# A hybrid decoder layer on one core: dt by column groups, and the samples' new states from stacked fp32r halves

## What is computed

```
u    = RMSNorm(x)
proj = u @ W_in                      # 2048 x 9248: z | xBC | dt (32 columns) | glu
dt   = softplus(dt_raw + dt_bias)    # one value per token and head, 32 heads
xBC  = SiLU(conv4(xBC)) -> x (32 heads of 64), B and C (4 groups of 128 states)
SSD scan, by heads:
  y = C h (decayed) + ((C B^T) * decay * dt) x
  new state of each sample and head: decay * h0 + sum_j B_j (decay_to_end * dt)_j x_j^T
  g = (y + D x) * SiLU(z), and group RMSNorm of g
conformer: GLU -> conv31 -> LayerNorm -> swish
x = x + RMSNorm(concat(ssd, conformer) @ W_out);  x = x + RMSNorm(W_down relu(W_up RMSNorm(x))^2)
```

## Time and profile before

| | |
|---|---|
| median of 3 runs | 1800.94 us |
| profiled execution, its own time | 1800.39 us |
| its span | 1798.8 us |
| PE (TensorE) busy | 1779.2 us, 99% |
| DVE (VectorE) busy | 1088.6 us, 61% |
| ACT (ScalarE) busy | 770.2 us, 43% |
| POOL (GpSimd) busy | 453.2 us, 25% |
| granted TensorE clock | 1.00 of full |
| DMA | 278.42 MB, 155 GB/s |

### The profile page before, as it was taken

The page is one execution under the profiler, slowest core; times in us unless marked ns, Lnnn a source line. Parts: engine busy times, 40 slices in busy tenths (PEclk is TensorE's granted clock), DMA queues, the critical chain, the costliest instruction groups (busy, mean ns, idle before and its releaser), DMA issues.

```text
span 1798.8 us, 34945 instructions
## 1 busy us (share of the span) xinstructions
PE 1779.2 (99%) x13213; PEld 1746.5 (97%) x13213; DVE 1088.6 (61%) x2004; ACT 770.2 (43%) x1139; POOL 453.2 (25%) x352
## 2 busy tenths in 40 slices
PE   8999999999999999999999999999999999999998
PEld 7999999999998898899899999999999999999998
DVE  5577887999788787865875333443434434344444
ACT  6443435555356565633443333333333333333442
POOL 1577776777651122222100000000000000000132
PEclk9999999999999999999999999999999999999999
DMA  8665554555545555564335444444444454444442
GB/s 252 176 189 153 145 157 139 149 152 153 153 144 165 161 177 163 163 215 152 117 123 166 156 140 140 157 156 155 140 140 153 156 158 140 140 151 158 154 143 87
DMA packets 287354, 278.42 MB, mean 155 GB/s; under 512 B 11639, under 2 KB 284767, under 8 KB 286385
## 3 DMA queue, kind: packets, MB, share of 16 engines
q1 hardware_dynamic: 249112, 247.87, 45.4%
q10 hardware_dynamic: 36496, 21.77, 4.1%
q0 software_dynamic: 1648, 7.43, 1.3%
HBM read 261.25 MB, written 17.22 MB: 155 GB/s over the span
## 4 chain that ended last, share of the span: by engine, by line
PE 94%; ACT 2%; DVE 2%; DMA 0%; issue 0%; ACTq 0%; SPq 0%; DVEq 0%
PE ps L1804 28%; PE ps L1806 28%; PE ps L1805 28%; PE ps L1863 1%; PE ps L2087 1%; PE ps L1865 1%; PE ps L1864 1%; PE ps L2060 1%; PE ps L2037 1%; PE ps L2131 1%; PE ps L2132 1%; PE ps L2133 1%; DMA xn<-in_x_prompt 0%; DVE mix L1671 0%; ACT wgt L988 0%
## 5 line engine op out<-in xcount | busy, mean ns | idle before, releaser
L1804 PE MATMUL ps<-ahi,whi 128*128 128x320 f32 x2304 | 717.8, 312 | 0.0
L1806 PE MATMUL ps<-ahi,wlo 128*128 128x320 f32 x2304 | 711.9, 309 | 0.0
L1805 PE MATMUL ps<-alo,whi 128*128 128x320 f32 x2304 | 711.8, 309 | 0.0
L677 ACT ACTIVATE whi<-raw 128x1024 fp32r<-128x1024 f32 (+1 forms) x467 | 479.5, 1048 | 448.6 <-PE ps L1806 382.9
L1205 DVE TENSOR_TENSOR wlo<-raw,whi 128x1024 fp32r<-128x1024 f32 x347 | 424.2, 1245 | 242.4 <-ACT whi L677 239.7
L1804 PEld LDWEIGHTS ps<-ahi,whi 128*128 128x128 f32 x2304 | 432.5, 188 | 1.7
L1805 PEld LDWEIGHTS ps<-alo,whi 128*128 128x128 f32 x2304 | 432.6, 188 | 0.5
L1806 PEld LDWEIGHTS ps<-ahi,wlo 128*128 128x128 f32 x2304 | 432.5, 188 | 0.0
L1804 PE MATMUL ps<-hhi,whi 128*128 128x320 f32 x1016 | 314.3, 309 | 0.0
L1806 PE MATMUL ps<-hhi,wlo 128*128 128x320 f32 x1016 | 313.9, 309 | 0.0
L1805 PE MATMUL ps<-hlo,whi 128*128 128x320 f32 x1016 | 313.9, 309 | 0.0
(11 more groups left out here) (316 smaller groups left out, 1626.3 us busy)
## 6 DMA issues: line engine op xcount, KB each, us to landing
raw<-in_w_in SPq DMA_DIRECT2D x144, 512.0 KB, 3.7
raw<-in_w_up SPq DMA_DIRECT2D x128, 512.0 KB, 4.5
raw<-in_w_down SPq DMA_DIRECT2D x128, 512.0 KB, 4.5
raw<-in_w_out SPq DMA_DIRECT2D x64, 512.0 KB, 3.8
h<-in_state_ssm ACTq DMA_DIRECT2D x16, 512.0 KB, 4.9
out<-hout ACTq DMA_DIRECT2D x16, 512.0 KB, 3.2
x_transposed<-xt ACTq DMA_DIRECT2D x1, 2560.0 KB, 10.1
xr<-x_transposed POOLq DMA_DIRECT2D x1, 2560.0 KB, 9.9
```

The costliest lines, as they stand in the source:

```text
L677: act.activation(whi[:, kq, :, 0:width], raw[:, kq, :, 0:width], ACT.Copy).then_inc(hi_done, 1)
L1804: pe.matmul(out, wh, hi[:, kk, :], start=(kk == 0), stop=False)
L1805: pe.matmul(out, wh, lo[:, kk, :], start=False, stop=False)
L1806: last = pe.matmul(out, wl, hi[:, kk, :], start=False, stop=(kk == NT - 1))
```

## The change

- **dt**: the four dt pieces go. `wdt` (128 x 16 blocks x 32 columns) is loaded in one DMA, VectorE scales it by the norm's weight, and TensorE multiplies it in plain fp32 with `xt0`: 16 products of 320 columns, the k-th in column group k mod 4 of the array. ScalarE copies the four partial sums (`dsum`), and one more product with a folded identity (`dfold`) adds them into bank 5 after the first granule of `glu(1)`.
- The store of `xt0` is issued by GpSimd in four parts. A split of GLU goes from GpSimd to VectorE.
- **New states of the samples**: L2087's two products become two fp32r matmuls with K = 128: in each, rows 64 to 127 hold the high part of `xdd` against all of B masked, rows 32 to 63 the high part again against B's low part, rows 0 to 31 the low part against B's high part. ScalarE makes four small copies per tile (`xq`), VectorE two small subtractions.
- **B's rows** `bq` (two buffers) are made a group ahead: TensorE turns B's last chunk in tile j = 1, ScalarE copies it (`b_rows`), makes 8 masked copies in tile j = 2 (`b_masked`), and 8 + 2 more in tile j = 3 (`b_low`, `b_high`). For the first group all of it is done in the first tile, with the 8 masked copies on VectorE. `bm` goes.
- `bt` and `xst` go: TensorE reads `xb` itself.
- The reciprocal of tile j = 2 is done in two halves: one at its old place, one after the tile's last product.

```diff
@@ TensorE, start
-            for kq in range(4):
-                first_piece(8 + kq, kq, 4, 1)
+            pe.wait_ge(x_copied, NT)
+            pe.wait_ge(wdt_done, 1)
+            for k in range(NT):
+                own = slice(HEADS * (k % 4), HEADS * (k % 4) + HEADS)
+                last = pe.matmul(ps[own, 4, 0:TOK], wdt[:, k, :], xt0[:, k, :], start=(k < 4), stop=(k >= NT - 4))
+            last.then_inc(dt_mm, 1)
+            def fold_dt():
...
+                pe.matmul(ps[0:HEADS, 5, 0:TOK], dfold[:, 0:HEADS], dsum[:], start=True, stop=True
+                          ).then_inc(dt_summed, 1)
@@ TensorE, scan_back
+                if j == 1 and i < 3:
+                    pe.wait_ge(exp_done, 2 * T + 1)
+                    pe.transpose(ps[:, 3, TOK:448], xb[:, NT + i + 1, TOK - P:TOK], ident[:]).then_inc(bts_trans, 1)
...
                 pe.wait_ge(h0t_ready, T + 1)
-                pe.wait_ge(bm_ready, i + 1)
+                pe.wait_ge(xq_ready, 2 * T + 2)
+                pe.wait_ge(bq_ready, 2 * i + 2)
                 for h in range(2):
-                    own_rows = slice(64 + 32 * h, 96 + 32 * h)
-                    pe.matmul(ps[:, 6 + h, :], xdd[own_rows, 2, :], bm[own_rows, 4 * h:4 * h + 4, :],
-                              start=True, stop=True)
+                    pe.matmul(ps[:, 6 + h, :], xq[h][:], bq[i % 2][:, 4 * h:4 * h + 4, :], start=True, stop=True)
@@ ScalarE, wc
                     if j == 0:
                         act.wait_ge(bt_trans, i + 1)
+                        if first:
+                            b_rows(ps[64:P, 4, 256:384])
...
+                    act.wait_ge(xd_ready, T + 1)
+                    if not first:
+                        act.wait_ge(st_done, T)
+                    for h in range(2):
+                        act.activation(xq[h][64:P, :], xdd[64:P, 2, :], ACT.Copy).then_inc(xhi_done, 1)
+                    for h in range(2):
+                        last = act.activation(xq[h][32:64, :], xdd[64 + 32 * h:96 + 32 * h, 2, :], ACT.Copy)
+                    last.then_inc(xq_ready, 1)
+                    if first:
+                        b_low(0)
                     if not first:
                         act.wait_ge(hnew_done, T)
...
                     act.activation(hts[:], ps[:, 4, 384:512], ACT.Copy).then_inc(hts_ready, 1)
+                    if first:
+                        b_high(0)
                     decay(T, 1)
+                    if j == 1 and i < 3:
+                        act.wait_ge(bts_trans, i + 1)
+                        b_rows(ps[64:P, 3, TOK:448])
...
-                    if j == 3 and not final:
-                        stage_b(i + 1)
-                    if not (final and j == 3):
-                        stage_x(T + 1)
+                    if j == 2 and i < 3:
+                        b_masked(i + 1)
+                    if j == 3 and i < 3:
+                        b_low(i + 1)
+                        b_high(i + 1)
@@ VectorE, wc
-                        dve.tensor_tensor(bm[:], btok[:, 2, :].unsqueeze(1).to_broadcast([P, NB, P]),
-                                          blk[:].unsqueeze(2).to_broadcast([P, NB, P]), ALU.mult
-                                          ).then_inc(bm_ready, 1)
+                        if first:
+                            b_lowest(0)
+                            dve.tensor_tensor(bq[0][64:P, :, :], ...)      # 64 x 1024
+                    if j == 2 and i < 3:
+                        b_lowest(i + 1)
...
-                        gate_scale(i - 1)
+                        gate_scale(i - 1, 0, TOK // 2)
...
+                    dve.wait_ge(xhi_done, 2 * T + 2)
+                    for h in range(2):
+                        own = slice(64 + 32 * h, 96 + 32 * h)
+                        last = dve.tensor_tensor(xq[h][0:32, :], xdd[own, 2, :], xq[h][own, :].bitcast(F32), ALU.subtract)
+                    last.then_inc(xq_ready, 1)
...
+                    if j == 2 and i >= 1:
+                        gate_scale(i - 1, TOK // 2, TOK)
+            def b_rows(transposed):
+                act.activation(bts[64:P, :], transposed, ACT.Copy)
+                act.activation(bthi[64:P, :], transposed, ACT.Copy).then_inc(bts_ready, 1)
+            def b_masked(i):
+                for b in range(NB):
+                    last = act.activation(bq[i % 2][64:P, b, :], bts[64:P, :], ACT.Copy, scale=blk[64:P, b:b + 1])
+            def b_low(i):
+                for b in range(NB):
+                    own = slice(64 + 32 * (b // 4), 96 + 32 * (b // 4))
+                    last = act.activation(bq[i % 2][32:64, b, :], btlo[own, :], ACT.Copy, scale=blk[own, b:b + 1])
+            def b_high(i):
+                for h in range(2):
+                    own = slice(64 + 32 * h, 96 + 32 * h)
+                    last = act.activation(bq[i % 2][0:32, 4 * h:4 * h + 4, :],
+                                          bq[i % 2][own, 4 * h:4 * h + 4, :].bitcast(F32), ACT.Copy)
```

More of the change, by code:

```diff
@@ L203, in build @@
                place("sqb2", [P, 4, TOK], at=sm + 1920)]
-        t1 = place("t1", [P, 2, TOK], at=own)
+        dsum = place("dsum", [P, TOK], at=own)
+        dfold = place("dfold", [P, 2 * HEADS], at=own + 320)
+        wdt = place("wdt", [P, NT, HEADS], at=own + 1056)
         ss = place("ss", [P, 4], at=own + 640)
@@ L340, in load @@
                 sp.dma_start(raw[:, kq, :, 0:width], src).then_inc(raw_ready[kq], 16)
[L342 to L346 removed]
+            for s in range(8):
+                kq, col = s // 2, (COL_GLU + D, COL_GLU)[s % 2]
                 if s == 2:
@@ L704, in first_split @@
             def first_split(s):
-                split(s // 4, s % 4, 256 if s < 8 else HEADS)
+                split(s // 4, s % 4)
             def first_halves(h):
@@ L816, in glu @@
                         v_rows(i - 1)
+            ahead(Q_GLU, 0, 6)
             sigmoid(0)
+            ahead(Q_GLU, 0, 7)
             act.wait_ge(par_trans, 1)
@@ L826, in _ @@
                            ).then_inc(par_done, 1)
-            first_split(10)
-            first_split(11)
-            ahead(Q_GLU, 0, 6)
-            ahead(Q_GLU, 0, 7)
-            dt_part(0)
+            act.wait_ge(dt_mm, 1)
+            act.activation(dsum[:], ps[:, 4, 0:TOK], ACT.Copy).then_inc(dt_copied, 1)
             act.wait_ge(par_done, 1)
@@ L1502, in _, with gate_scale @@
             xt3 = ps[:, 4, 0:384].rearrange("p (c h d) -> p c h d", c=3, h=2)
-            def gate_scale(g):
+            def gate_scale(g, lo=0, hi=TOK):
                 dve.wait_ge(rooted, 3 + g)
-                dve.reciprocal(gss[:, g, :], gss[:, g, :]).then_inc(gn_root, 1)
+                last = dve.reciprocal(gss[:, g, lo:hi], gss[:, g, lo:hi])
+                if hi == TOK:
+                    last.then_inc(gn_root, 1)
             def gate_mult(g):
@@ L1859, in first_piece @@
                             pe.wait_ge(act_ready, kk + 1)
-                        cols = slice(n * P, (n + 1) * P) if s < 8 else slice(0, HEADS)
-                        out = ps[0:P if s < 8 else HEADS, bank + n, 0:TOK]
-                        wh, wl = whi[:, slot, k, cols], wlo[:, slot, k, cols]
+                        out = ps[:, bank + n, 0:TOK]
+                        wh, wl = whi[:, slot, k, n * P:(n + 1) * P], wlo[:, slot, k, n * P:(n + 1) * P]
                         pe.matmul(out, wh, ahi[:, kk, :], start=(kk == 0), stop=False)
@@ L1899, in turn_xconv_states @@
                 pe.wait_ge(sst_in, 16)
+                pe.wait_ge(dt_act, 1)
                 if h:
@@ L1935, in glu @@
                         c = 4 * p + kq
+                        if second and c == 0:
+                            fold_dt()
                         if second:
@@ L2020, in scan_front @@
                         hi = min((c + 1) * P, TOK)
-                        last = pe.matmul(ps[:, 2, c * P:hi], bt[:, off:off + P], xb[:, NT + GROUPS + i, c * P:hi],
+                        last = pe.matmul(ps[:, 2, c * P:hi], xb[:, NT + i, off:off + P], xb[:, NT + GROUPS + i, c * P:hi],
                                          start=True, stop=True)
@@ L2026, in scan_front @@
                     pe.wait_ge(pst_done, T)
-                pe.wait_ge(xst_ready, T + 1)
                 for c, off in enumerate((0, P, TOK - P)):
-                    last = pe.transpose(ps[:, 4, c * P:(c + 1) * P], xst[:, off:off + P], ident[:])
+                    last = pe.transpose(ps[:, 4, c * P:(c + 1) * P], xb[:, T, off:off + P], ident[:])
                 last.then_inc(xtile_trans, 1)
+                if j == 2 and i < 3:
+                    pe.wait_ge(bts_ready, i + 2)
                 segment(T, 0, first)
```

109 lines of the change are left out of this document (62 added, 47 removed).

## The result

| | before | changed |
|---|---|---|
| median of the runs | 1800.8 us (1800.57 to 1800.97) | 1817.8 us (1809.25 to 1821.01) |
| ratio | | 1.0089, 95% interval 1.0079 to 1.0099 |
| profiled execution: own time, span | 1800.39, 1798.8 us | 1817.08, 1815.5 us |

The forecast was 1800.8 us, with a chance of 0.53 for no change and 0.21 for slower. The time itself is now spread over 12 us (six runs), where that of the kernel before has 0.4. The two profiled executions are 16.7 us apart; where these went is read from their profiles. Experiments are compared by their medians.

A forecast was written before the change was run, and what follows sets the result against it. TensorE's instruction stream plus few short waits was taken as the bound. Terms -4.0 ordinary tiles, -4.0 dt, +3.8 tile 0, +1.4 and +2.4 late tiles, +0.3 transposes sum to -0.1 us: 1800.8 us, range 1793 to 1805.5.

The forecast's parts named there:

- Rival 3: dt: column groups take turns, so its products take 8.6 us for 6.97; 1807.0 us, slower; chance 0.07.
- I cost the SyncE and GpSimd queues at nothing: Start: one 256 KB load for four of 64 KB and four stores for one, same bytes, add 0 us.
- the price if the cover fails: Behind dt: if weights of `glu(1)` asked for earlier still come late, TensorE waits one piece, about 3.5 us.
- ScalarE's copies: Scan: small copies cost 0.8 us a tile, free in ordinary tiles; tile 0 loses 3.8 us with the first group's.
- more than 5 us after its old distance: Tile 0: forecast wrong if L1560 comes under 2.5 or over 5 us after its old distance from the tile's start.
- the late tiles: Tiles 5, 9, 13 add 0.8 us each and 8, 12 add 0.7 each, ScalarE's chain being late: +2.4 and +1.4.
- the waits at `within()`: Scan: TensorE's waits there for VectorE's last product rise from 2.5 to some 12 us, about 0.25 per ordinary tile.
- the ordinary tile: Ten scan tiles gain 0.40 us each, 4.0 in all; TensorE waits at `within()` for the rest of 0.66.
- `xq` coming late: Tiles 7, 11, 15: `xq` is ready some 0.2 us before its matmul; cost nothing, at the end 0.3 us.
- The +0.3 us for the transposes: Scan: three added transposes of B and their change of order cost 0.3 us in all.
- Rival 1: Scan: the saving stays whole, no hold by the decay chain and ScalarE's copies free; 1786.6 us; chance 0.05.
- Rival 4: Scan: ScalarE bounds every tile if a small copy costs over 0.33 us; 1813.9 us at 0.46; chance 0.06.

The follow-up runs named there:

- start_back: Changed kernel with x stored once by ScalarE's queue after the last tile and the small dt weights loaded behind the last input-weight piece; 1810.5 us.
- dt_fixed: Kernel before with the dt part alone, one x store by ScalarE's queue and the dt weights behind piece 7; 1796.8 us, 0.9981.
- dt_only: Kernel before with only the dt part and GpSimd's x stores, old scan over the samples, reciprocal whole; 1804.2 us (1797.0 to 1806.0).
- warm0: Changed kernel with 40 more bf16 matmuls, never read, at the head of the scan's first tile to keep TensorE busy; 1819.4 us.
- first_group: Changed kernel with the first group's rows of B made by VectorE and GpSimd in place of ScalarE; 1811.4 us.
- best3: Kernel of best, with the copies of x's rows left to ScalarE in tiles 7, 11 and 15; 1796.5 us, 0.9979 of before.
- best: Changed kernel with both DMAs put back, first masked rows early on VectorE, other x and B row copies on GpSimd; 1798.5 us, 0.9988.
- best2: Kernel of best, with the rows of B for groups 1 to 3 left with ScalarE; 1798.2 us (1796.2 to 1800.8).
- best_whole: Kernel of best, with the gate's reciprocal in one piece again in the third tile of groups 1 to 3; 1801.7 us.
- pool_xq: Changed kernel with the four copies of x's rows per tile moved from ScalarE to GpSimd; 1809.6 us (1807.8 to 1811.1).

## Why the prediction was wrong

**dt: the size right, its cover wrong.** The column groups took 2.29 us (2.4 forecast; the ends were 2.2 and 8.6), 3.8 times faster than the 8.6 us for the 32 in turn. With the fold's 0.66 us the gain is 4.02 us, 4.0 forecast. My estimate from the Trainium skill's page "TensorE: Matmul & The Clock Gate", section "Measured speedup vs the span model", was 2.7 us; the measured time is shorter. The rule of its section "The mechanism", that a weight load overlaps matmuls in flight only when the row group differs, does not fit here: the earlier trace rows already had weight loads busy for 97% of the span beside matmuls for 99%. Rival 3 is out. What failed is the step "I cost the SyncE and GpSimd queues at nothing". I argued with the sum of the bytes and not with when they move: two of the four stores of 640 KB (issued at 25.5 and 33.8 us, landed at 36.4 and 46.7) run beside the loads of pieces 6 and 7 (23.1 to 37.5 us and 27.6 to 45.0). I did name the price if the cover fails, 3.5 us for one piece; it was 5.6 us, and I gave it no place in the chances. start_back (7.3 us under the changed kernel) and dt_fixed (7.4 under dt_only) show it: about 7 us of the 17.0 are this step, with the half clock behind the wait.

**The clock: left out.** No term of the sum had it. At the start the half clock cost 2.7 us; in tile 0 of the changed kernel nothing (warm0). Half clock in tiles 13 and 14 costs 1.1 to 1.5 us each time, in the changed kernel, in first_group and in best3, where no wait of over 1.6 us stands before it. It falls on other tiles from kernel to kernel (the profiles of best, best2 and best_whole have none in the scan). All kernels with the scan's part have a spread of 2 to 12 us, against 0.4 to 1.0 for the one before and 1.8 for dt_fixed; that the half clock makes this spread is not shown. Why it falls there stays open.

**ScalarE's copies: the term that was mis-sized.** I took 0.18 to 0.2 us for one of `xq` and 0.26 for one of `b_low`, from a 128-partition copy out of PSUM and from decays. Measured from start to start: the four of `xq` 562.94 - 561.76 = 1.18 us a tile (0.8), `b_low` 2.56 (2.1), `b_high` 1.29 (1.0). Within `xq` only the first copy cost what I took, 0.22 us (561.76 to 561.97); the next, up to the first copy into other partitions, 0.31, and those two 0.32 and 0.33. The sum in tile 0 is 5.0 for 3.8: L1622 comes 5.2 us later after the tile's start than before, and tiles 0 and 1 together lost 5.4. The prediction's own sign of being wrong, "more than 5 us after its old distance", was thus met. In tiles 8 and 12 it is +1.3 (0.7), in 5 and 9 +1.4 and +1.1 (0.8). pool_xq shows that it is these copies: without them on ScalarE the four are within 0.15 us of before.

**A wait that I had not named.** In the late tiles TensorE now waits at `hts`, ahead of `within()`. I had looked only at VectorE's last product; the same ScalarE delay reaches TensorE sooner. It is the same term, not a second price: the waits at `within()` come to 5.7 us where I had forecast some 12, and with the 5.1 us for `hts` to 10.8.

**Right, in part:** the ordinary tile. Tiles 2, 3 and 10 gain 0.38 to 0.39 us for 0.40, and TensorE waits at `within()` there, 0.16 us for the 0.25 forecast. Tiles 4, 6, 7, 11 and 15 gain only 0.20 to 0.29; in the last three the term that I had put at nothing, `xq` coming late, costs 0.1 us each. The +0.3 us for the transposes (tiles 1, 5 and 9) was not measured apart. Rival 1 (saving whole) is out. Rival 4 was nearest in mechanism: the four copies cost 0.30 us each on average, just under the 0.33 from which every tile would have lost. Its 0.06 was too low when I had written that at 0.3 us a copy the sum was +3.

By terms in the profiled run, with the forecast's transposes at 0.1 us in each of tiles 1, 5 and 9: start and way to the scan +5.0 (forecast -4.0), tiles 0 and 1 +5.4 (+3.5), the five late tiles +7.6 with 1.2 of half clock in tile 13 (+4.0), the other nine -1.3 with 1.5 of half clock in tile 14 (-3.6): +16.7 against -0.1.

## What to carry to other kernels

A DMA that is moved is priced by what is in flight beside it and by the slack of the next load, not by its bytes: here one alone was free, the other cost 0 to 3 us, and both together cost 7. Small copies on an engine that is idle half of the time cost the full sum wherever that engine's chain ends last, so read their price from a row with the same partitions and source, or give them to an engine that is not in the chain. And where TensorE is the bound, look at the granted clock behind each new long wait: the waits of 3.1 to 6.4 us behind TensorE's first matmuls all had half clock with them here, at a price between nothing and 2.7 us.

## What was not expected of the hardware

- Either of two DMAs alone left piece 7's split at 36.0 or 38.0 us, both together put it at 45.0, but at 38.8 in dt_only's profile; in ten runs of that kernel the time fell on either side of a gap (1797.0 and 1797.8 against 1802.6 to 1806.0).
- With a wait of 3.13 us of TensorE added to the kernel before, the granted clock was 0.5 for 6.8 us, from 0.5 us after the wait's begin.
- GpSimd's copy of 64 x 128 took 0.29 us alone and 1.63 when VectorE's two-input product of 1.48 us had just started; VectorE's own subtraction of 32 x 128 took 0.28 alone and 1.81 beside GpSimd's product of 1.89. In both rows the engine that started second ended 0.14 to 0.15 us after the other.
- Two ScalarE copies of 128 columns into the same partitions started 0.22 us apart, copies of the same length into other partitions 0.32 us.
